# Neighbourhood attention of a fused transformer kernel: projections by seven half-size products, weight sums on GpSimd, gate by tanh, bias without its zeros

## What is computed

```python
def neighbourhood_mixer(u_lat, u_ctx, w_in, w_out, qn_g, kn_g, rpb, need_ctx):
    q, k, v, z = jnp.split(u @ w_in, 4, axis=-1)      # u: 512 tokens, and 256 of context
    q, k = rms_norm(q, qn_g), rms_norm(k, kn_g)       # per head of 64
    # queries of a block of 16 columns see a band of 32 columns, 8 rows: 256 keys
    s = einsum(q_r, k_band) * scale + bias            # bias -1e30 outside the window
    s_ctx = einsum(q_r, k_c) * scale                  # 256 keys of the context, no bias
    p = softmax(concatenate([s, s_ctx]))
    o = einsum(p_band, v_band) + einsum(p_ctx, v_c)
    return (o * silu(z)) @ w_out
```

## Time and profile before

| | us |
|---|---|
| median of 3 runs | 4011.27 (4003.71 to 4012.37) |
| the profiled execution, its own time | 4011.99 |
| its span in the trace | 4010.3 |
| PE busy, share of the span | 3700.1 (92%) |
| DVE busy | 2045.9 (51%) |
| ACT busy | 1197.8 (30%) |
| GpSimd (POOL) busy | 143.2 (4%) |
| L1188, projections of both attention kinds: PE busy | 634.1 |

### The profile page before, as it was taken

The page is one execution under the profiler, slowest core; times in us unless marked ns, Lnnn a source line. Parts: engine busy times, 40 slices in busy tenths (PEclk is TensorE's granted clock), DMA queues, the critical chain, the costliest instruction groups (busy, mean ns, idle before and its releaser), DMA issues.

```text
span 4010.3 us, 44586 instructions
## 1 busy us (share of the span) xinstructions
PE 3700.1 (92%) x16234; PEld 2354.2 (59%) x16234; DVE 2045.9 (51%) x3693; ACT 1197.8 (30%) x2200; POOL 143.2 (4%) x227
## 2 busy tenths in 40 slices
PE   5998999998889999899999999998798999999989
PEld 2445488873446888665656565564454555555554
DVE  3744353644545545455666666666214555555541
ACT  1213210112332101133434434343102454545530
POOL 6600000000000000000000000000000000000000
PEclk8998999999999999999999999999899999999999
DMA  7521334340013342410111011100011122212211
GB/s 149 143 75 48 95 95 106 89 112 24 21 53 105 95 116 74 116 37 27 32 31 31 26 31 31 31 26 26 23 51 58 53 58 58 58 53 57 58 32 53
DMA packets 456433, 246.27 MB, mean 61 GB/s; under 512 B 44256, under 2 KB 448352, under 8 KB 456320
## 3 DMA queue, kind: packets, MB, share of 16 engines
q1 hardware_dynamic: 420384, 216.15, 19.6%
q0 software_dynamic: 14144, 28.36, 2.7%
q10 hardware_dynamic: 21792, 0.22, 0.4%
HBM read 229.83 MB, written 14.80 MB: 61 GB/s over the span
## 4 chain that ended last, share of the span: by engine, by line
PE 79%; DVE 12%; ACT 4%; issue 2%; ACTq 1%; DMA 0%; DVEq 0%; SPq 0%
PE bank L466 19%; PE bank L1188 15%; PE bank L328 10%; PE bank L1709 8%; DVE rs L1934 4%; PE bank L1695 3%; PE bank L1036 3%; PE bank L1100 3%; PE bank L863 2%; PE bank L1731 2%; PE bank L1081 2%; PE bank L1742 2%; PE bank L846 1%; PE bank L1677 1%; PE bank L1345 1%
## 5 line engine op out<-in xcount | busy, mean ns | idle before, releaser
L1188 PE MATMUL bank<-hT,ring 128*128 128x512 f32 (+1 forms) x1664 | 634.1, 531 | 11.3 <-ACT hT L1599 6.0
L1709 PE MATMUL bank<-hT,ring 128*128 128x512 f32 x1504 | 509.0, 490 | 20.0 <-DVE big L1961 16.3
L1188 PEld LDWEIGHTS bank<-hT,ring 128*128 128x128 f32 x1664 | 311.1, 191 | 289.0 <-issue 276.2
L1709 PEld LDWEIGHTS bank<-hT,ring 128*128 128x128 f32 x1504 | 280.6, 190 | 244.4 <-issue 207.1
L328 PE MATMUL bank<-big,ring 128*128 128x512 f32 (+1 forms) x1024 | 389.2, 543 | 12.3 <-DVE big L1973 8.4
L328 PEld LDWEIGHTS bank<-big,ring 128*128 128x128 f32 x1024 | 195.8, 192 | 204.2 <-issue 183.9
L1088 ACT ACTIVATE arena<-bank 128x512 f32<-128x512 f32 (+2 forms) x224 | 118.4, 528 | 462.3 <-PE bank L1081 462.0
L466 PE MATMUL bank<-big,arena 128*128 128x256 f32 x1024 | 228.8, 379 | 0.0
L466 PEld LDWEIGHTS bank<-big,arena 128*128 128x128 f32 x1024 | 194.6, 190 | 26.5
L1056 DVE CUSTOM_DVE_ANT_0 arena<-bank,big 128x512 f32<-128x512 f32 (+2 forms) x152 | 101.3, 666 | 201.4 <-PE bank L1036 201.4
L1695 PEld LDWEIGHTS bank<-ring,hT 128*128 128x128 f32 x1536 | 179.2, 193 | 30.4 <-DVE arena L1928 17.1
(11 more groups left out here) (293 smaller groups left out, 5276.0 us busy)
## 6 DMA issues: line engine op xcount, KB each, us to landing
ring<-in_mlp_w SPq DMA_DIRECT2D x128, 512.0 KB, 5.5
ring<-in_a_w_in SPq DMA_DIRECT2D x64, 512.0 KB, 4.0
ring<-in_b_w_in SPq DMA_DIRECT2D x64, 512.0 KB, 4.0
ring<-in_mod_w SPq DMA_DIRECT2D x48, 512.0 KB, 4.0
ring<-in_even_w_in SPq DMA_DIRECT2D x32, 512.0 KB, 4.0
bias_d<-tb POOLq DMA_DIRECT2D x96, 128.0 KB, 3.3
big<-bias_d POOLq DMA_DIRECT2D x16, 768.0 KB, 5.4
ring<-in_a_w_out SPq DMA_DIRECT2D x16, 512.0 KB, 3.7
```

The costliest lines, as they stand in the source:

```text
L1188: mm = pe.matmul(bk(b + n)[0:m, 0:z - a], ring[s][:, k, 0:m], (rhs or hcol)(k, a, z), start=k == 0, stop=k == kt - 1)
L1709: mm = pe.matmul(flatb[2][:, a:z], ring[s][:, k, :], hT[:, k, a:z], start=k == 0, stop=k == KT - 1)
```

## The change

**Projections.** The slabs q and k are one pair of output tiles, v and z another. For the 512 tokens each pair is now seven products P1 to P7 of four matmuls with 256 columns (`n_products`, L2188); the context's k and v stay as they were, 16 matmuls of 256 (`n_context`, L2207). The differences T1 to T4 of the tokens are made once, ahead of the layer, by DVE (`dve_nat_sums`). The sums S1 to S4 of a pair's weights are made by GpSimd (`n_weights`, L2238), 8 a pair of heads. Results lie in two accumulators `two[0]`, `two[1]` over banks 2 and 3, and the context's in bank 2 between them.

**Copies.** ACT copies P1 and P5 out (L2218). DVE adds the blocks (L2262, L2272, L2276, L2280, L2292 to L2296) and copies the context (L2301, L2306). ACT copies the first half of v in its bands (`n_values`, L2255), into the room that k, still to be scaled, held.

**Order.** The entries of the slots are other ones; q's square and column sum move to slot 3, its root to slot 4. The last transposes of v and the tanh move to slot 0 of the next turn (`nat.open`).

**Gate.** tanh(z/2) on ACT (L2414), one scalar_tensor_tensor on DVE in slot 4 (L2365), and the factor 0.5 in the last product (L2114).

**Bias.** Rows of 256 without zeros, and one stretch of 256 zeros; `masked_band` gives the maximum a view of both.

```diff
@@ nat
+        nsum = {S1: tb[...], S2: part(6656, S), S4: part(8704, S), S3: cz}
+        NPROD = {P1: ("A11", B11, "C"), P5: (S1, T1, "Y"), P6: (S2, T2, "X"), P4: ("A22", T4, "Z"),
+                 P2: ("A12", B21, "C"), P3: (S4, B22, "Y"), P7: (S3, T3, "X")}
+        def n_products(r, xs):
+            def f(pe, ph, g, e, u):
+                for x in xs:
+                    if x == P1:
+                        pe.wait_ge(m_free, nth("free", 2, g, r))
+                    if x == P5 and r == 1:
+                        pe.wait_ge(ph.gd, g * 2 + 2)
+                    if wt in nsum:
+                        pe.wait_ge(m_wsum, nth("wsum", 8, g, 4 * r + wt))
+                    if x == P6:
+                        pe.wait_ge(m_copied, nth("copied", 4, g, 2 * r + 1))
+                    if x == P4:
+                        pe.wait_ge(m_copied, nth("copied", 4, g, 2 * r + 2))
+                    if x == P2:
+                        pe.wait_ge(m_u2, nth("u2", 2, g, r + 1))
+                    if x == P7:
+                        pe.wait_ge(m_c11, nth("c11", 2, g, r + 1))
...
+        def n_weights(pool, r, g, e, u):
+            for x in (S1, S2, S4, S3):
+                pool.wait_ge(m_prod, nth("prod", 14, g, 7 * (r - 1) + {S1: P5, S2: P6, S4: P3, S3: P7}[x]))
...
+                pool.tensor_tensor(nsum[x], i0, i1, op).then_inc(m_wsum, 1)
+        def n_values(act, ph, g, e, u):
+            act.wait_ge(m_prod, nth("prod", 14, g, 7 + P2))
+            act.wait_ge(ph.nr, g * 2 + 2)
+            for t in (0, 2):
+                m = act.activation(n_v[:, t:t + 2, 0:4], two_bands(two[1].C, t), ACT.Copy)
+            m.then_inc(m_c11, 1)
...
+        def n_ctx_v(dve, ph, g, e, u):
+            dve.wait_ge(ph.cv, g + 1)
+            dve.wait_ge(ph.vt, g * 3)
+            dve.tensor_copy(n_vc, bk(2)[:, C:2 * C]).then_inc(ph.gd, 1)
...
+        nat.pe = [n_products(0, (P1, P5)), n_products(0, (P6, P4)), n_products(0, (P2, P3)),
+                  both_(n_products(0, (P7,)), st_pe(0), n_context(1)), n_context(2),
+                  both_(st_pe(1), n_products(1, (P1, P5))), both_(st_pe(2), n_products(1, (P6, P4))),
+                  both_(n_products(1, (P2,)), vt_pe("vc"), n_products(1, (P3, P7)), vt_pe("v0"))]
+        nat.act = [both_(n_copied(0, P1), n_copied(0, P5)), nothing, nothing, sq_act(0), both_(std_act(0), sq_act(1)),
+                   both_(sq_act(2), std_act(1), n_copied(1, P1), n_copied(1, P5)), std_act(2),
+                   both_(n_values, vt_act("vc"), vt_act("v0"))]
+        nat.dve = [nothing, n_u2(0), n_first_tile(0), n_second_tile(0), both_(qn_dve, n_ctx_k, n_ctx_v), kl_dve,
+                   both_(n_u2(1), kn_dve), both_(n_first_tile(1), n_second_tile(1))]
@@ attend, dve
-                    if on and u == 0 and ph.late:
+                    if on and u == 4 and ph.late:
```

More of the change, by code:

```diff
@@ L1114, in attend @@
             for u in range(8):
+                if u == 0 and g is not None and ph.first:
+                    ph.first(who, eng, g, ge, gu)
                 if who == "pe":
@@ L2078, in program, with masked_band @@
         n_rawq = part(6144, 512)
-        n_v = flat[:, 11776:13056]
-        bias = [flat[:, o:o + 3072].rearrange("p (v n) -> p v n", v=6) for o in (8192, 13056)]
-        n_z = flat[:, 11264:11776]
+        n_z = flat[:, 11520:12032]
+        n_vc = flat[:, 15360:15616]
+        n_v = part(7168, 4 * C).rearrange("p (t r x) -> p t r x", t=4, r=ROWS)
+        NB, NZERO = 8192, 11264
+        bias = [flat[:, NB + 1536 * e:NB + 1536 * e + 1536].rearrange("p (v n) -> p v n", v=6) for e in range(2)]
+        zero = flat[:, NZERO:NZERO + C]
         BAND0 = (0, 8, 24, 32)
+        def masked_band(e, n):
+            o = NB + 1536 * e + C * n
+            return flat[:, o:o + 2 * (NZERO - o)].rearrange("p (a n) -> p a n", a=2)[:, :, 0:C]
         def grid(x):
@@ L2121, in sq_act, with nth @@
[L2121 to L2128 removed]
+        def nth(name, per, g, n):
+            return g * per + (2 * M_TOTAL[name] + n)
+        nsum = {S1: tb[:, :, :].rearrange("p a b -> p (a b)")[:, 0:S], S2: part(6656, S), S4: part(8704, S), S3: cz}
@@ new lines, in program, with __init__ @@
+        n_t = {x: flat[:, o:o + 4 * H] for x, o in ((T2, 12288), (T3, 13312), (T4, 14336))}
+        np1, np5 = tb[:, :, :].rearrange("p a b -> p (a b)")[:, S:S + H], flat[:, 16128:16384]
+        nu2, nu3 = part(9216, H), flat[:, 12032:12288]
+        class Two:
+            def __init__(self, r):
+                self.r = r
+                b = [bk(2 + r), bk(3 - r)]
+                self.C, self.X, self.Y, self.Z = b[0][:, 0:H], b[0][:, H:S], b[1][:, 0:H], b[1][:, H:S]
+        two = [Two(0), Two(1)]
@@ new lines, in n_context, with f @@
+        def n_context(j):
+            def f(pe, ph, g, e, u):
+                s = 4 * e + j
+                arrived(pe, "nat", s, u)
+                if j == 1:
+                    pe.wait_ge(m_u3, nth("u3", 2, g, 1))
+                    if isinstance(g, int) and g == 0:
+                        pe.wait_ge(u_c, 2 * KT)
+                for k in range(KT):
+                    mm = pe.matmul(bk(2)[:, C * (j - 1):C * j], ring[s][:, k, :], hT[:, k, S:TT],
+                                   start=j == 1 and k == 0, stop=k == KT - 1, skip_group_check=True)
+                mm.then_inc(slab_done[s] if j == 1 else nat.cv, 1)
+            return f
@@ new lines, in n_second_tile, with f @@
+        def n_second_tile(r):
+            def f(dve, ph, g, e, u):
+                w = two[r]
+                dst = an(e, 2560, 512) if r else n_raw
+                if r == 0:
+                    dve.wait_ge(ph.vt, g * 3)
+                dve.wait_ge(m_prod, nth("prod", 14, g, 7 * r + P7))
+                dve.tensor_tensor(nu3, np1, w.X, ALU.add).then_inc(m_u3, 1)
+                dve.wait_ge(m_u3, nth("u3", 2, g, r + 1))
+                dve.wait_ge(m_copied, nth("copied", 4, g, 2 * r + 2))
+                dve.tensor_tensor(dst[:, 0:H], nu3, w.Z, ALU.subtract).then_inc(m_free, 1)
+                dve.tensor_tensor(dst[:, H:S], nu3, np5, ALU.add).then_inc(m_c2, 1)
+            return f
@@ L2187, in f @@
                 free5(pe, ph, g, x)
-                for k in range(*VT[x]):
-                    j = k - VT[x][0]
-                    mm = pe.transpose(bk(5)[:, P * j:P * j + P], n_v[:, P * k:P * k + P], ident)
+                k0, k1 = VT[x]
+                for k in range(k0, k1):
+                    src = part(7168 + P * k, P) if k < 8 else n_vc[:, P * (k - 8):P * (k - 7)]
+                    mm = pe.transpose(bk(5)[:, P * (k - k0):P * (k - k0) + P], src, ident)
                 mm.then_inc(ph.vt, 1)
```

228 lines of the change are left out of this document (158 added, 70 removed).

## The result

| | before | after |
|---|---|---|
| median, us (runs) | 4011.82 (4) | 4063.49 (4) |
| lowest to highest | 4003.71 to 4012.41 | 4053.39 to 4067.13 |
| ratio, with its 95% interval | 1 | 1.013 [1.0107, 1.0153] |
| profiled execution, own time; span | 4011.99; 4010.3 | 4067.13; 4065.5 |
| PE busy, us (share of the span) | 3700.1 (92%) | 3679.0 (90%) |

The change makes the kernel 1.3% slower: 52 us by the medians, 55 between the two profiled executions, where I had forecast 25. One run of a later kernel (old_gate) is left out of its figures: it took 4508.98 us at a mean granted clock of 0.829, where the others of that kernel have 0.966 or 0.967. The steady part first, in the same window as the earlier trace rows. Columns: length, busy (instructions) of PE, PEld, DVE, ACT, POOL, granted clock, DMA share, GB/s.

What follows compares the result with a forecast made beforehand. PE bounds the kernel before; afterwards a serial chain through ACT and DVE was to bound it. 4012.0 - 8 (start) + 32 (turns) + 4.5 (GpSimd) - 3 (end) = 4037.5, so 4037 us by the median; range 4004 to 4078.

Steps and rivals of the forecast that it cites:

- The turn: Steady loop of the layer: a closed serial chain makes a turn 54.0 us, 2.2 more than the 51.8 before.
- Q: The end of the scores of tile 2 in slot 3 of a turn, from which the new chain is counted.
- 32 and 4.5: Cost over 15 turns: +32 us from the longer chain, +4.5 from GpSimd's additions holding up DVE.
- a rival of 15%: PE standing 3.0 us each turn lowers its clock, losing 1.8 a turn: +27, 4064 us; chance 15%.
- The start: From the layer's opening to its first scores, expected at 3073 to 3076: -8 us.
- The end: From the last pair's first scores to the next layer: DVE's gate work leaves, tanh and others come in; -3 us.
- GpSimd: Eight weight additions a turn beside DVE: 0.3 us a turn, 4.5 in all; rival 2.4 a turn, 4073 us, chance 8%.
- S4's meeting with k's scaling: On the chain, GpSimd's sum S4 falls on DVE's scaling of k and maximum 7.
- three meetings: GpSimd additions beside DVE on the chain, each costing between 0 and 0.9 us; 0.3 a turn taken in all.
- Outside the layer: The stages ahead of the layer and behind it: no change, 0 in the forecast.
- without any new wait 47.5 us: A turn if no wait held: 51.8 - 3.4 - 0.8; as part of the faster rival 3937 us, chance 5%.
- the lost wait's 0.8: PE's only large idle time in a turn of the kernel before, 0.81 us ahead of a transpose.

Runs made afterwards that it cites:

- old_gate: The changed kernel with the gate as before (exponential, addition of 1, reciprocal, product) at the new gate's place in slot 4; 4094.52 us, ratio 1.0224.
- wait_filled: The changed kernel with PE kept busy ahead of P7 by 18 useless transposes a turn, nothing taken off the chain; 4046.09 us, ratio 1.0085.
- sums_twice: The changed kernel with each of GpSimd's weight sums made twice, once more into a spare buffer; 4064.5 us, ratio 1.0143.
- opening: The changed kernel with ACT's first copies of P1 and P5 ahead of its context shifts, and DVE's differences ahead of the context's reciprocal; 4041.07 us, ratio 1.0083.
- six_moves: five_moves with the output products one slot later on DVE and, in the opening, P6's partial sum ahead of the context; 3930.1 us, ratio 0.9804.
- tanh_alone: The kernel before with only the gate changed to tanh, one DVE instruction and a factor 0.5 in the output products; 4006.56 us, ratio 0.9992.
- square_early: The changed kernel with q's square on ACT in slot 2 instead of slot 3; 4073.79 us, ratio 1.0162.
- five_moves: three_moves with q's square in slot 2 and v's transposes put off to slots 0 and 1 of the next turn; 3956.35 us, ratio 0.9876.
- context_first: The changed kernel with DVE's copies of the context's k and v ahead of q's reciprocal instead of behind its scaling; 4067.94 us, ratio 1.0152.
- root_early: The changed kernel with q's root on ACT in slot 3 instead of 4 and DVE's gate product in slot 5; 4015.27 us, ratio 1.001.
- v_spare: The changed kernel with v's first block copied by ACT into a spare buffer ahead of exponential 7 and arranged in bands later; 4024.24 us, ratio 1.0039.
- three_moves: The changed kernel with root_early, v_spare and opening together; 3975.39 us, ratio 0.9927.

## Why the prediction was right and wrong

- **The turn: right.** I had 54.0, of which 25.0 from Q to P7, 18.9 + 3.6 + 6.5 back to the next Q. Measured: 54.27. In the turn of the chain printed above, tile 2's scores end, and Q is, at 3547.36. q's reciprocal starts at Q + 4.1 (forecast 4.1), the context's copies end at Q + 8.9 (9.1), k's root at Q + 12.9 (13.1), the last root at Q + 19.6 (20.0), P7 starts at Q + 24.9 (25.0). Full-clock turns cost 36.6 over 15 (wait_filled), where the sum had 32 and 4.5. That these agree so closely is luck: the 4.5 were for GpSimd, which cost nothing here, and the chain itself is 0.3 a turn longer than I added up, all of it between P7 and the next Q (29.4, where I had 29.0).
- **The step that failed first: the clock, set aside as a rival of 15% instead of a term of the sum.** I had the row for it: after 2.88 us of idle time in the earlier trace rows, 1.8 us lost. And the sum itself said that PE would stand 3.0 us each turn. I kept it out because another idle time, of 2.70, had been followed by full clock. The answer was neither: some turns lost 1.4 to 3.0 us, others nothing. In the change it is 15.1 us over the turns.
- **The start: -8, measured -0.6.** P1 came as forecast (10.3 us behind the column sums; I had 10.2). But I let P5 start 1.5 too early. It waits for two of DVE's differences of the tokens, and beside GpSimd's first sums, which are made at the same time, each takes up to 2.17 us; the last one, with no addition beside it, takes 1.23. DVE's second and last, then the addition that lies beside the second and third:

```profile
3040.43 2.17 DVE L2447 TENSOR_TENSOR hT<-hT 128x1024 f32<-128x1024 f32 x1
...
3044.84 1.23 DVE L2447 TENSOR_TENSOR big<-big,hT 128x1024 f32<-128x1024 f32 x1
```

```profile
3041.48 2.25 POOL L2238 TENSOR_TENSOR cst<-ring 128x512 f32<-128x512 f32 x1
```

The two ahead of P5 took 4.24 (2.07 and 2.17) instead of 2.46. That is enough for the 1.5, and it is contention, which I had priced in the turns and not here; no run leaves the sums out, so this rests on the durations and on sums_twice. P6 I had right behind P5, at the low clock. It waited 4.77 for ACT, whose copies are queued behind its eight shifts of the context, and those behind DVE's four differences and the context's scaling. I had followed the data and not ACT's queue. The opening experiment gives 3.5 back; in six_moves the stretch is 50.80, 9.6 shorter than before.

- **The end: -3, measured 0.0.** The work did leave (tanh_alone: 28.52 against 32.34), and the clock took it back. In this stretch PE does short pieces with waits of up to 1.2 us between them. square_early, whose end is the same code with the same waits, is at full clock up to the next layer and takes 26.16; the change takes 32.33 at a granted clock of 0.72 to 0.89, and wait_filled 29.84. Of wait_filled (0.72 and 0.5) and of square_early (1.00):

```profile
3903.00:3909.00 6.00, 4.46 (x28) 2.83 (x23) 2.69 (x10) 1.96 (x6) 0.00 (x0) 0.72 0.00 0
3921.00:3927.00 6.00, 4.30 (x26) 3.00 (x24) 0.19 (x1) 1.20 (x2) 0.00 (x0) 0.50 0.00 0
```

```profile
3922.00:3928.00 6.00, 4.16 (x40) 2.95 (x40) 3.42 (x11) 2.73 (x6) 0.00 (x0) 1.00 0.01 3
```

The kernel before is not at full clock there either (0.57 from 3864 to 3870), so the -3 compared two ends at clocks that I had not looked at.

- **GpSimd: +4.5 in the turns, measured 0; nothing at the start, measured 1.8 ahead of P5.** In the turns the meetings exist and are dear: a scaling of probabilities on DVE takes 1.53 to 1.56 us instead of 0.49. But in the change's order the one that is hit stands where DVE has time. S4's meeting with k's scaling, which I had put on the chain, came as said, and GpSimd took it: the scaling takes its 1.02, the addition 1.53 instead of 1.27. I priced three meetings by thirds of a row when I could have looked which DVE instruction is due while each sum runs. In five_moves one of them did lie on PE's path.
- **Outside the layer: 0, measured +2.1 and +1.9.** Scatter between executions, as the study's other profiles show.

Together: 15.1 for the clock in the turns, 3.0 at the end, 7.4 at the start, 4.0 outside, and 0.1 in the terms of the turn. They make the 29.6 us between the forecast sum of 4037.5 and the profiled execution of 4067.13. Chain, places of the waits and turn were right. The sum lacked what a wait of 3 us does to the matmuls behind it, and the order of ACT's and GpSimd's work at the start.

The term "without any new wait 47.5 us" came within 0.3: six_moves runs at 47.22. That fits seven products worth their 3.4 us and the lost wait's 0.8, hidden in the change by the order on ACT and DVE: six_moves has PE do the same work in another order. The bias without its zeros had no run of its own; the maximum that reads it takes 0.68 as before. Whether the old products in a new order of ACT would come below 51.0 was not tried; in a turn of 51.8 the kernel before has only about 1 us in which PE does not work (1.06 of 60 in the earlier trace rows).

## What to carry to other kernels

When matmuls are taken away from an engine that was the bound, add up the serial chain of the small steps behind it in the new program order, engine by engine: it decides, and it can be predicted to a few tenths from rows of the old trace. Price a wait by what the closed loop loses, not by its length (1.47 us were worth 0.25, and nothing), and put the clock into the sum as soon as TensorE is to stand some 3 us in every turn. Where work moves to GpSimd, look which DVE instruction runs beside it, at the start as well as in the loop. Judge a part on the kernel that it goes into: in the turns the tanh gate is worth nothing alone and 3.75 us each here.

## What the hardware showed

**The clock's fall depends on more than the wait.** In the turns the granted clock fell behind waits of 3.71 us every time (old_gate), behind 2.8 to 2.9 in 7 of 15 turns (the change), 4 (opening), 5 (sums_twice), 8 (context_first) and 14 (square_early), behind 2.6 in 6 (root_early), and never where the longest wait was 1.5 or less (v_spare, three_moves, five_moves, wait_filled). From the second turn on, one that is hit lost 1.4 to 3.0 us. The same wait with the same work around it is hit in one turn and spared in the next, so such a kernel's turns scatter and no single one tells the mean. But 1.5 us is no safe length elsewhere: at the layer's end the clock fell to 0.72 and 0.5 with no wait above 1.2 us (wait_filled, shown above), and with the same waits it did not in square_early.

**DVE held up by GpSimd.** DVE's scaling of 512 probabilities, one input and one output in SBUF, takes 1.55 instead of 0.49 where it starts together with a GpSimd addition. From five_moves, DVE and then GpSimd:

```profile
3336.32 1.55 DVE L1077 TENSOR_SCALAR arena<-arena,cols 128x512 f32<-128x512 f32 x1
```

```profile
3336.33 1.27 POOL L2248 TENSOR_TENSOR cst<-ring 128x512 f32<-128x512 f32 x1 [0.81 <-PE bank L2196]
```

1.55 is the 1.27 of the addition and 0.28 of the scaling behind it. In sums_twice, where the scaling starts 0.78 after an addition, it takes 0.78 and ends 0.29 behind the addition's end: DVE waits for the whole instruction, it does not share. The Trainium skill says so ("SBUF — State Buffer", section "SBUF: two separate sides"): the pair of ports that both use is an exclusive lock for the length of an instruction, and the other one blocks. The trace agrees. Which of the two came first in five_moves, 0.01 us apart, the records can't tell.

DVE's partial sum with one input from PSUM, beside an addition for nearly all of its length, takes its usual 0.42. From the change:

```profile
3197.70 0.42 DVE L2262 TENSOR_TENSOR arena<-tb,bank 128x256 f32<-128x256 f32 x1 [3.23 <-PE bank L2188]
```

```profile
3197.73 1.27 POOL L2238 TENSOR_TENSOR arena<-tb,ring 128x512 f32<-128x512 f32 x1 [0.82 <-PE bank L2188]
```

Where both run without a pause, as at the layer's start, both grow: DVE's differences to 2.17 from 1.23, GpSimd's additions to 2.06 and 2.25 from 1.26.
